# Two edits in a two-block kernel: the order at the end of the first stage, and loads, banks and engine split of the mLSTM recurrence

## What is computed

```python
        xs = causal_depthwise_conv(lx, sc_w[l], sc_b[l])
        xh = xs.reshape(bsz, seq, LRU_HEADS, LRU_HEAD_DIM)
        r = jax.nn.sigmoid(jnp.einsum("bshd,hde->bshe", xh, wr[l]).reshape(bsz, seq, D_LRU) + br[l])
        i = jax.nn.sigmoid(jnp.einsum("bshd,hde->bshe", xh, wi[l]).reshape(bsz, seq, D_LRU) + bi[l])
...
        a = jnp.exp(log_a)
        mult = jnp.sqrt(-jnp.expm1(2.0 * log_a))
        bx = mult * (i * xs).astype(jnp.float32)
        hs = linear_scan(a, bx).astype(x.dtype)
        y_lru = hs * jax.nn.silu(ls)
```

```python
        C_new = a[..., None, None] * C + jnp.einsum('bhs,bhsd,bhse->bhde', ws, kc, vc)
...
        dmat = jnp.where(tri, b[..., :, None] - b[..., None, :] + li[..., None, :], -jnp.inf)
...
        s = jnp.einsum('bhtd,bhsd->bhts', qc, kc) * jnp.exp(dmat - m_t[..., None])
        num = w_inter[..., None] * jnp.einsum('bhtd,bhde->bhte', qc, C) + jnp.einsum('bhts,bhse->bhte', s, vc)
        den = w_inter * jnp.einsum('bhtd,bhd->bht', qc, n) + jnp.sum(s, axis=-1)
        h = num / jnp.maximum(jnp.abs(den), jnp.exp(-m_t))[..., None]
```

## Time and profile before

| what | value |
|---|---|
| median of 3 runs | 2136.63 us (2135.2 to 2137.69) |
| profiled execution | 2136.5 us |
| its span in the trace | 2134.7 us |
| PE busy | 2031.3 us, 95% |
| DVE, ACT, POOL busy | 60%, 38%, 45% |
| mean granted clock of PE | 0.97 |

### The profile page before, as it was taken

The page is one execution under the profiler, slowest core; times in us unless marked ns, Lnnn a source line. Parts: engine busy times, 40 slices in busy tenths (PEclk is TensorE's granted clock), DMA queues, the critical chain, the costliest instruction groups (busy, mean ns, idle before and its releaser), DMA issues.

```text
span 2134.7 us, 23884 instructions
## 1 busy us (share of the span) xinstructions
PE 2031.3 (95%) x9072; PEld 1667.7 (78%) x9072; DVE 1270.9 (60%) x1370; ACT 803.6 (38%) x1010; POOL 966.0 (45%) x540
## 2 busy tenths in 40 slices
PE   4999999999999999999998998988999999999997
PEld 3788788887788888878886877766888888788874
DVE  7789998878542476546402785488655555613137
ACT  4342356565442313221232344445444333402132
POOL 1375745555222222233311116557877788722262
PEclk7999999999999999999997999998999999999998
DMA  9641112122112332548654955241222222153132
GB/s 374 196 151 34 48 49 72 55 72 72 40 60 79 119 109 70 172 120 308 218 165 131 313 181 163 84 148 60 60 60 60 89 80 79 60 197 127 36 101 101
DMA packets 268670, 251.40 MB, mean 118 GB/s; under 512 B 8258, under 2 KB 230211, under 8 KB 268563
## 3 DMA queue, kind: packets, MB, share of 16 engines
q1 hardware_dynamic: 265475, 238.42, 35.4%
q10 hardware_dynamic: 3088, 11.54, 1.4%
HBM read 206.08 MB, written 43.84 MB: 117 GB/s over the span
## 4 chain that ended last, share of the span: by engine, by line
PE 49%; issue 14%; DVE 5%; POOL 3%; DMA 1%; ACT 1%; SPq 1%; ACTq 0%; POOLq 0%; DVEq 0%
PE PS L2109 17%; PE PS L1657 15%; PE PS L2001 5%; PE PS L1896 5%; POOL wl L815 2%; PE PS L2123 2%; DVE B L2888 1%; PE PS L1954 1%; PE PS L1819 1%; PE PS L1947 1%; PE PS L1948 1%; PE PS L2035 1%; PE PS L1909 1%; DVE B L2887 1%; DMA SCR<-um_d 0%
## 5 line engine op out<-in xcount | busy, mean ns | idle before, releaser
L815 POOL TENSOR_TENSOR wl<-raw,wh 128x1024 fp32r<-128x1024 f32 (+1 forms) x157 | 378.4, 2411 | 824.9 <-ACT wh L1044 602.6
L1657 PE MATMUL PS<-XH,wh 128*128 128x512 f32 x1424 | 443.5, 393 | 8.3 <-POOL wl L815 2.8
L1657 PE MATMUL PS<-XH,wl 128*128 128x512 f32 x1424 | 441.2, 391 | 0.0
L1657 PE MATMUL PS<-XL,wh 128*128 128x512 f32 x1424 | 440.5, 391 | 0.0
L1657 PEld LDWEIGHTS PS<-XH,wh 128*128 128x128 f32 x1424 | 268.0, 189 | 67.5 <-issue 4.5
L1657 PEld LDWEIGHTS PS<-XH,wl 128*128 128x128 f32 x1424 | 269.3, 189 | 56.4
L1657 PEld LDWEIGHTS PS<-XL,wh 128*128 128x128 f32 x1424 | 268.9, 189 | 56.2
L1044 ACT ACTIVATE wh<-raw 128x1024 fp32r<-128x1024 f32 (+1 forms) x108 | 111.0, 1028 | 440.2 <-PE PS L1657 187.5
L2321 DVE SCALAR_TENSOR_TENSOR PS<-B,PJ,PS 128x1022 f32<-128x1022 f32 (+7 forms) x197 | 251.1, 1275 | 7.5
L1114 ACT ACTIVATE wh<-raw 128x1024 fp32r<-128x1024 f32 x48 | 50.8, 1058 | 263.8 <-PE PS L1657 248.8
L975 POOL TENSOR_TENSOR wl<-SCR,wh 128x512 fp32r<-128x512 f32 x80 | 114.1, 1428 | 70.5 <-ACT wh L1496 70.5
(11 more groups left out here) (412 smaller groups left out, 3750.4 us busy)
## 6 DMA issues: line engine op xcount, KB each, us to landing
B<-in_ada_w SPq DMA_DIRECT2D x48, 512.0 KB, 5.3
raw<-in_ffn_up_w SPq DMA_DIRECT2D x48, 512.0 KB, 4.3
raw<-in_w_in SPq DMA_DIRECT2D x40, 512.0 KB, 4.9
raw<-in_m_in_w SPq DMA_DIRECT2D x37, 512.0 KB, 5.0
mod_tiles<-in_mod_w SPq DMA_DIRECT2D x16, 512.0 KB, 13.0
raw<-in_w_out SPq DMA_DIRECT2D x16, 512.0 KB, 4.8
qkvo_d<-B SPq DMA_DIRECT2D x16, 512.0 KB, 3.5
raw<-in_m_out_w SPq DMA_DIRECT2D x16, 512.0 KB, 4.1
```

What stands on the lines that cost most here:

```text
L815: tt(wl[slot][:, 0:kc, :], raw[slot][:, 0:kc, :], wh[slot][:, 0:kc, :].bitcast(F32), ALU.subtract).then_inc(lo_done, 1)
L1657: last = mm(ps[:, c:c + step_n], W[:, k, :], Y[:, k, c:c + step_n], start=(seen == 0), stop=(seen == total - 1))
```

## The change

It has two parts. At the end of the first stage, for the last head alone: POOL makes the low part of the gate weights ahead of `xsL`, and DVE makes `xsL`; PE's gates run pass by pass and wait for `xsL` before their third pass only; ACT's silu of `ls` and its table load stand behind the square root; the last six convolution steps of DVE stand behind its low parts for G1; and one tile is counted that does not exist, so that G1's tiles change banks. In the recurrence: the second slot of direction 0 lies elsewhere, and the loads of chunk 1 stand ahead of the last projection store; later loads wait for fewer stores; the two banks of transposes and scores change places; ACT hands a bank over before its scaling copy; the mask is added by POOL for four heads at once and the column is taken off by ACT as the bias of four exponentials; POOL normalises the first four tiles of the readout. The diff, cut:

Constants and banks, which all engines share:

```diff
-        L1 = Product(KD, 5 * KD, 6 * KD)
+        L1 = Product(KD, 5 * KD, 6 * KD + 1)
-        DVE_HIGH = 3
+        DVE_HIGH = 4
-        G1 = Product(KD)
+        G1 = Product(KD, tiles=KD + 1)
-        H_PS = (0, 1, 0, 2, 3, 2, 3, 2)
+        H_PS = (1, 0, 1, 2, 3, 2, 3, 2)
-            for slot, (buf, off) in enumerate(((SCR, d * n_loaded), (flat, HQ))):
+            second_slot = (2 * ALL, HQ)[d]
+            for slot, (buf, off) in enumerate(((SCR, d * n_loaded), (flat, second_slot))):
+        KT_BANK = G5.T % 2
+        KT, QK = PS[KT_BANK][:, 0:HQ], PS[1 - KT_BANK][:, 0:HQ]
```

On SP, at the end of the projections:

```diff
             for t in range(Gx.n - 1, Gx.n + 1):
-                unit(GxG.U + t + 2, (GxG.U + t) % 2, cols_of(m_out_w, 0, KD, (t - Gx.n + 1) * P))
+                half_unit(t - Gx.n + 1)
+                if t == Gx.n:
+                    sp.wait_ge(*at("late_summed", LATE * KD))
+                    sp.wait_ge(*at("late_ps", 1))
+                    for d in range(2):
+                        chunk_load(1, d, 1, False)
                 proj_store(t - V_UNITS, t % 2)
+            for s in range(2):
+                sp.wait_ge(*at(f"proj_out{s}", 16 * len(range(s, QK_TILES + 1, 2))))
+            for n in range(2, 4):
+                for d in range(2):
+                    chunk_load(n, d, n % 2)
```

On POOL, in the first stage:

```diff
             for i in range(KD):
-                pool.wait_ge(*at("xsh", i + 1))
-                tt(xsL, xs_t, xsH.bitcast(F32), ALU.subtract).then_inc(ev("xsl"), 1)
                 gates_low(i)
+                if i < KD - 1:
+                    pool.wait_ge(*at("xsh", i + 1))
+                    tt(xsL, xs_t, xsH.bitcast(F32), ALU.subtract).then_inc(ev("xsl"), 1)
```

On POOL, in the recurrence:

```diff
-            with pool.Fori(0, NT // 2) as i:
-                for u in range(2):
-                    for d in range(2):
-                        q2(2 * i + u, d, u)
+            def masked(j, d, slot):
+                M_t = M[d]["slots"][slot]["M"]
+                pool.wait_ge(*at(f"chunk_in{d}{slot}", 48 * ((j + NC) // 2) + 48))
+                tt(M_t, M_t, mask[d][:].rearrange("p (o t) -> p o t", o=1).to_broadcast([P, HEADS, P]), ALU.add).then_inc(ev("d_ok"), 1)
+            READ_AT = {NT + 5: (0,), NT + 6: (1,), NT + 7: (2, 3)}
+            for y in range(2 * NT):
+                j, d = divmod(y, 2)
+                masked(j, d, j % 2)
+                q2(j, d, j % 2)
+                if y == 4:
+                    low(G5.U + 1, (G5.U + 1) % 2)
+                for n in READ_AT.get(y, ()):
+                    read_norm(n)
```

On ACT, from the first stage to the recurrence:

```diff
-                act.sem_inc(taken[0], 1)
+                act.sem_inc(taken[0], 1 if i < KD - 1 else 2)
+                gates_high(i)
                 xs_high(i)
-                gates_high(i)
                 if last:
-                    f(spare[:], eps[:], ACT.Silu)
-                    ls_evac(i)
-                    hi(ls_unit(i) + 2)
-                    for k in range(DVE_HIGH, KD - 2):
-                        lru_high(k)
+                    lru_high(KD - 4)
                 act.wait_ge(*at("m2", i + 1))
                 f(th_t, th_t, ACT.Sqrt).then_inc(ev("mult_ok"), 1)
...
+            lru_high(KD - 3)
+            ls_evac(KD - 1)
+            hi(ls_unit(KD - 1) + 2)
...
                 f(B2[:, t, :], PS[b][:], ACT.Copy).then_inc(taken[b], 1)
+                if t == KD - 1:
+                    act.sem_inc(taken[1 - b], 1)
...
                 step.wait()
+                act.sem_inc(taken[b], 1)
                 if scale is not None:
                     step.link(f(stage[s][:, CTX:ALL], stage[s][:, CTX:ALL], ACT.Copy, scale=scale))
                 act.sem_inc(ev("proj_sb"), 1)
-                act.sem_inc(taken[b], 1)
...
-                if seq:
-                    act.wait_ge(*at("d_ok", y + 1))
-                    f(m["M"], m["M"], ACT.Exp, scale=-1.0).then_inc(ev("e_ok"), 1)
+                act.wait_ge(*at("d_ok", y + 1))
+                for h in range(HEADS):
+                    ins = f(m["M"][:, h, :], m["M"][:, h, :], ACT.Exp, scale=-1.0, bias=gate_col(COLS, 0, n, d)[:, h:h + 1])
+                ins.then_inc(ev("e_ok"), 1)
```

On PE:

```diff
-                pe.wait_ge(*at("xsl", i + 1))
+                pe.wait_ge(*at("xsh", i + 1))
...
-                for c, ps in enumerate((PS[2], PS[b])):
-                    for n, (W, Y) in enumerate(((g_wh, xsH), (g_wl, xsH), (g_wh, xsL))):
+                for n, (W, Y) in enumerate(((g_wh, xsH), (g_wl, xsH), (g_wh, xsL))):
+                    if n == 2:
+                        pe.wait_ge(*at("xsl", i + 1))
+                    for c, ps in enumerate((PS[2], PS[b])):
...
-                        pe.wait_ge(*at("yT_ok", 2 if b else 3))
+                        pe.wait_ge(*at("yT_ok", 3 if b == KT_BANK else 2))
```

On DVE:

```diff
+                if i == KD - 1:
+                    dve.wait_ge(*at("xsh", i + 1))
+                    V.tensor_tensor(xsL, xs_t, xsH.bitcast(F32), ALU.subtract).then_inc(ev("xsl"), 1)
                 if i:
                     lru(i - 1)
-                conv_steps(CONV_AT[i], CONV_AT[i + 1])
+                if i < KD - 1:
+                    conv_steps(CONV_AT[i], CONV_AT[i + 1])
...
+            lru_scan(KD - 1)
+            g1_low(KD - 3)
             g1_low(KD - 2)
-            lru(KD - 1)
+            lru_gate(KD - 1)
             g1_low(KD - 1)
+            conv_steps(CONV_AT[KD - 1], CONV_AT[KD])
...
-                if seq:
-                    dve.wait_ge(*at(f"chunk_in{d}{slot}", 48 * k + 48))
-                    for h in range(HEADS):
-                        ins = stt(out=m["M"][:, h, :], in0=m["M"][:, h, :], scalar=col(COLS, 0, n, d)[:, h:h + 1], in1=mask[d][:], op0=ALU.subtract, op1=ALU.add)
-                    ins.then_inc(ev("d_ok"), 1)
...
-                if w == 3:
-                    read_norm(0)
-                    read_norm(1)
-                if w in (5, 6):
-                    read_norm(w - 3)
+                if w in (3, 5):
+                    read_reciprocals(w - 3)
```

More of the change, by code:

```diff
@@ L734, in _ @@
                     chunk_load(n, d, n % 2)
+                if n > 4 and n - 5 < 4:
+                    gate_load(n - 5)
+            for t in range(2, 4):
+                half_unit(t)
             sp.wait_ge(*at("hs_ok", NT))
@@ L1356, in _ @@
                     f(ECOL, COLS[:, :, 2 * HEADS:NCOL], ACT.Exp).then_inc(ev("ecol"), 1)
+                    for d in range(2):
+                        context_weights(0, d)
                 high_at(GxG.U + O_UNIT + k + 1, 0)
@@ L1361, in weights @@
             def weights(k, slot, d, seq):
+                if not seq:
+                    return
                 m = M[d]["slots"][slot]
@@ L1408, in readout @@
                         read_high(n)
-            second(G5)
+            for d in range(2):
+                context_weights(1, d)
             recurrence(act, weights, heads, readout=readout)
@@ L1929, in scores @@
                     for h in range(HEADS):
-                        last = nc.tensor.transpose(PS[0][:, h * P:(h + 1) * P], m["k"][:, h, :], ident[:])
+                        last = nc.tensor.transpose(KT[:, h * P:(h + 1) * P], m["k"][:, h, :], ident[:])
                     last.then_inc(ev("t_ps"), 1)
@@ L1935, in scores @@
                     for h in range(HEADS):
-                        last = mm(PS[1][:, h * P:(h + 1) * P], m["k"][:, h, :], m["q"][:, h, :], start=True, stop=True)
+                        last = mm(QK[:, h * P:(h + 1) * P], m["k"][:, h, :], m["q"][:, h, :], start=True, stop=True)
                     last.then_inc(ev("s_ps"), 1)
@@ L2389, in _ @@
             V.tensor_tensor(th_t, th_t, r_t, ALU.mult).then_inc(ev("m2"), 1)
-            for k in range(DVE_HIGH, KD - 2):
-                g1_low(k)
+            g1_low(KD - 4)
             dve.wait_ge(*at("mult_ok", KD))
@@ L2671, in heads @@
                     r = rec_t[d][:]
[L2672 removed]
+                    step.link(stt(out=r, in0=DEN, scalar=-1.0, in1=gate_col(ECOL, 0, n, d), op0=ALU.mult, op1=ALU.max))
                     step.link(V.tensor_tensor(r, DEN, r, ALU.max))
```

76 lines of the change are left out of this document (47 added, 29 removed).

## The result

The changed kernel takes 2118.43 us in the median of 7 runs (2106.15 to 2120.61); the kernel before, measured beside it, 2136.63 us (2132.34 to 2140.82). The ratio is 0.9902, with a 95% interval of 0.9882 to 0.9923. The forecast was 2117.2 us with a range of 2109 to 2124.

A forecast was written before the change was run, and what follows sets the result against it. PE is busy nearly everywhere, so only its waits and lower clock can give time. Stage end -6.9, G2 wait +2.3, recurrence start -8.9, tail -6.3, G5 +0.5 sum to -19.3: 2136.5 becomes 2117.2 us, range 2109 to 2124.

The forecast's parts named there:

- Idle time ahead of the gates: First stage's end: PE's 4.06 us idle before the last head's gates go, and the gates take 2.67 us instead of 5.13.
- The step that keeps the three waits at 2.4 us: G1's first tiles: three waits for DVE's low parts, 2.4 us together, were kept unchanged in the sum.
- the hold-up that the prediction priced at 1.9 us: First stage's end: DVE's xsL and lows beside POOL risk a shared-port delay of 1.9 us each, left to the bounds.
- The prediction's floor: Gates to G1's third tile: PE's own work alone, 2.67 + 11.09 + 22.80 = 36.56 us, a gain of 10.1.
- Convolution steps at nothing: First stage's end: moving six DVE convolution steps behind the low parts for G1 was costed at nothing.
- The wait ahead of G2: G2's first matmul waits for ACT to empty G1's last tile: +2.3 us, bounds 1.0 and 4.8.
- Start of the recurrence: Up to step 6: earlier bank and chunk 1 loads, then chunk 2 late; gain 8.9 us, bounds 3 and 12.
- its first rival: Recurrence start: chunk 2 lands as late as before, gain falls from 8.9 to 3, time 2123 us; chance 0.17.
- The term that lets the 2.04 us for DVE go: Step 4 to step 6: the 2.04 us wait for DVE state updates queued behind masks goes, 14.22 us becoming 12.2.
- Masks and their price: Recurrence steps: POOL's mask addition takes 1.28 us, ACT's four exponentials 0.63 to 2.5; the PE-bound middle changes by 0.
- The rival with a slow form: Recurrence: POOL's mask addition with a repeated operand is slow, time above 2141 us; chance 0.03.
- Tail: Recurrence end: PE's 5.9 us of waits for DVE go, reciprocal 0.4 us sooner; gain 6.3, bounds 3 and 7.9.

The follow-up runs named there:

- run 8: Changed kernel with G2 on the other bank, DVE's low part of piece 5 ahead of the scan and ACT's high part of piece 6 ahead of a weight's: 2107.21 us.
- run 11: Changed kernel with DVE's last six convolution steps back ahead of the scan's chain, all else as changed: 2122.36 us.
- run 2: Kernel before with only the edits of the first stage's end, the recurrence as before: 2140.93 us beside 2137.24, ratio 1.0003.
- run 5: Changed kernel with the loads of chunk 1 put back behind the last projection store: 2126.13 us.
- the second trace: Profile of the changed kernel measured once more with no edit: span 2117.6 us; that measurement's median was 2119.33 us.
- Runs 6 and 7: Changed kernel with the masks back on DVE, normalisations on POOL: 2125.20 us; changed kernel with the first four normalisations back on DVE, masks on POOL: 2120.26 us.
- run 1: The changed kernel measured and profiled again, no edit: 2119.33 us, ratio 0.9903.

## Why the prediction was right, and where it was right by luck

The time came out 1.2 us from the forecast, and the local sum 1.3 us from the traces' -20.6. Point by point:

- **Idle time ahead of the gates: right.** It went, and the gates ran at full clock, 2.89 us busy where 2.67 were predicted. The wait for the cs tile's silu, predicted as 0.8, is 0.96 (L1220).
- **G1's opening: 1.2 us too hopeful.** The step that keeps the three waits at 2.4 us failed by size: 3.5 us are left, in two waits. DVE's scan stands ahead of the low part of piece 5, and ACT's table load and silu, which the prediction put "off PE's path", ahead of the high part of piece 6. By the timeline the second costs little: the low part of piece 6, which DVE makes from it, is itself stretched beside POOL, 2.67 us where that of piece 5 took 1.23, and these 1.4 us are most of PE's wait of 1.67 for it. This is the hold-up that the prediction priced at 1.9 us and left to its bounds; it struck once. In run 8 the same operation took 1.22 us, and all that the run took off is 1.5 us. From the changed kernel's timeline:

```profile
536.68 1.23 DVE L2422 TENSOR_TENSOR XL<-SCR,XH 128x1024 fp32r<-128x1024 f32 x1
537.66 2.49 POOL L827 TENSOR_TENSOR wl<-raw,wh 128x1024 fp32r<-128x1024 f32 x1 [11.39 <-ACT wh L1143]
538.56 2.67 DVE L2422 TENSOR_TENSOR XL<-SCR,XH 128x1024 fp32r<-128x1024 f32 x1 [0.66 <-ACT XH L1229]
541.29 0.74 PE L1864 MATMUL PS<-XH,wh 128*128 128x512 f32 x2 [1.67 <-DVE XL L2422]
```

- **What the tile counted in L1 is for: taken, not named.** The prediction's floor has 11.09 us of the ls window's 12.29; the rest is a wait of 1.21 us of G1's first matmul, which ended just behind the silu of `ls` on the bank that both used (540.58 us in the trace before). It is gone, though that silu now ends at 536.36, 7.2 us behind G1's opening at 529.16. No run leaves this tile out, so what it is worth is not measured.
- **Convolution steps at nothing: right**, and the most important order of the stage's end: run 11 lost 6.7 us there without it, in waits and in the clock, which the prediction did not say.
- **The wait ahead of G2: found, its clock under-weighed.** 2.19 us for 2.3. The forecast left the clock out because the stretch is about half of the one that showed a drop; six of seven traces show the drop behind it, 1.7 us. The high bound of 4.8 had it in. With it the end of the first stage is worth 1.8 us by its local terms and nothing that could be measured (run 2), where -4.6 was predicted. That is the term that failed by most, though the run's interval leaves room for a gain of up to 3 us.
- **Start of the recurrence: 11.3 or 9.1 us in the two traces, where 8.9 was predicted.** The mechanism (chunk 1's loads ahead, then chunk 2 late) is that of run 5. Chunk 2's load landed 7.06 us after its issue, 7.80 in the second trace, where the prediction took 7.1; its first rival, that it lands as late as before, fell in all eleven traces. (Before it landed after 10.7 us, and not after the 10.5 of the prediction.) The term that lets the 2.04 us for DVE go failed in its reason: a wait of 1.49 us stays at the same place, now for POOL's addition, ACT's four exponentials and the weighing in a row. In the second trace it is 0.15, as PE's own work there runs at the lower clock behind a longer wait for step 4's load. With the masks back on DVE the stretch is 11.64 us, between the 11.42 and the 11.83 of these two. What is shorter from step 4 to step 6 in the first trace, beside 0.5 us of this wait, is the clock: the trace before lost 1.7 us between 1180 and 1184. The row of hand-overs, from the changed kernel's timeline of step 4:

```profile
1154.14 1.27 POOL L951 TENSOR_TENSOR SCR<-SCR,mask 128x512 f32<-128x512 f32 x1 [17.86 <-DMA SCR<-um_d]
1155.45 1.28 ACT L1407 ACTIVATE SCR<-SCR,B 128x128 f32<-128x128 f32 x4 [0.78 <-POOL SCR L951]
1156.83 0.69 DVE L2703 TENSOR_TENSOR B<-PS,SCR 128x512 f32<-128x512 f32 x1 [1.39 <-ACT SCR L1407]
1157.96 1.14 PE L2003 MATMUL PS<-B 128*128 128x257 f32 x4 [1.49 <-DVE B L2713]
```

- **Masks and their price: right.** POOL's addition with a repeated operand takes 1.27 us, as L932 does, and the four exponentials 1.28 within the bounds of 0.63 and 2.5. The rival with a slow form fell.
- **Tail: right in size**, 5.8 for 5.8. The idle time did not go as far as was said, though: 1.3 us are left up to the last transposes, where under 1 was named as a sign, and 1.6 directly ahead of them; 1.0 of the 5.8 us is less busy time of PE. Runs 6 and 7 give the masks the larger part, and add that splitting the two kinds of work the other way (masks on DVE, normalisations on POOL) gains nothing over before.
- **The whole.** The recurrence alone gives 19.7 us where -14.7 was predicted, the stage's end alone none where -4.6 was: the two errors have opposite signs, and the forecast's nearness owes something to that. That is the luck in it. It owes something to the clock too: by the traces of run 1 the changed kernel without its clock loss is 12.8 us shorter than the kernel before (2073.5 for 2086.3; other pairs of traces differ by 4 to 6 us from what their edits do). The rest of the 18.2 us in the medians would then be less time at the lower clock, of which the prediction counted only the 2.5 at the gates.

## What to carry to other kernels

Where a producer's queue holds work for later, moving that work behind the consumer's inputs can be worth more than any single wait: here six convolution steps and six loads carried most of the gain at either place. When a count of tiles changes the parity of banks, look at the opening of the next product: the last tile of the old one may now hold the bank that is wanted, and the wait costs its length and, in six of seven traces here, what the clock loses behind it. Compare two traces stretch by stretch between the same instructions, and price the lower clock apart, before a difference is put down to an edit.

## What the runs showed of the hardware that was not expected

Two executions of one kernel differed by 12 us, and by as much in what they lost, by estimate, to the lower granted clock: 44.1 and 32.1 us, with 2073.5 left in both. Behind a wait of 2.19 us the clock fell in six of seven traces, behind one of 1.16 us in the single trace that has it, it did not. A DVE operation of 128x128 with two SBUF inputs, 0.35 us in the middle of the recurrence, took 1.09 us on average beside POOL's normalisations (4.36 for four). And DMAs of the same size landed 6.5 to 8.3 us after their issue, or 10.1 to 10.7 with six others issued just ahead of them.
